# Rotary halves exchanged by ScalarE copies instead of a TensorE rotation matmul, in the first block of a two-block model

## The reference, cut to what matters

```
def rope(x, pos):
    d = x.shape[-1]
    ...
    x1, x2 = jnp.split(x, 2, axis=-1)
    return jnp.concatenate([x1 * cos - x2 * sin, x2 * cos + x1 * sin], axis=-1)
```

## Time and profile before

| what | value |
|---|---|
| median of 3 runs | 2612.03 us (2608.58 to 2612.68) |
| the profiled execution | 2606.96 us, of it 2605.2 us span |
| TensorE busy | 94% of the span |
| VectorE, ScalarE, GpSimd busy | 70%, 51%, 16% |
| weights and the rest read from HBM | 362.60 MB |

### The profile page before, as it was taken

How to read it: one execution, slowest core, us unless ns; L and a number is a source line. 1 busy time by engine, 2 the same in 40 slices (tenths; PEclk the granted TensorE clock), 3 DMA queues, 4 the chain that set the end, 5 groups by cost and what they waited for, 6 DMA issues and landing times.

```text
span 2605.2 us, 50262 instructions
## 1 busy us (share of the span) xinstructions
PE 2459.5 (94%) x18862; PEld 2339.8 (90%) x18862; DVE 1817.3 (70%) x3451; ACT 1333.6 (51%) x2218; POOL 419.9 (16%) x548
## 2 busy tenths in 40 slices
PE   7999998999999999998999998999999988999998
PEld 6998997888999998997888998888999988889998
DVE  5698855666875689856676774876766558667664
ACT  5644455755544644455755545544444454344443
POOL 0000003617930000003526940000000000000000
PEclk9999998999999999999999998988999999899999
DMA  5432342344554433342334554432545543334553
GB/s 208 161 107 100 112 147 88 114 138 146 170 171 156 167 113 109 106 146 98 114 133 151 171 178 138 146 114 90 170 158 182 186 140 128 101 118 146 195 186 130
DMA packets 100432, 366.76 MB, mean 141 GB/s; under 512 B 11632, under 2 KB 12144, under 8 KB 99824
## 3 DMA queue, kind: packets, MB, share of 16 engines
q1 hardware_dynamic: 100208, 363.69, 41.8%
HBM read 362.60 MB, written 1.05 MB: 140 GB/s over the span
## 4 chain that ended last, share of the span: by engine, by line
PE 58%; DVE 18%; POOL 9%; DVEq 5%; ACT 4%; issue 3%; ACTq 1%; DMA 1%; SPq 0%; POOLq 0%
PE psum L450 58%; POOL ring_lo L1963 9%; DVE ring_lo L1282 4%; ACT arena L852 2%; ACT ring_hi L865 1%; DVE arena L1316 1%; DVE arena L1324 1%; DMA ring<-w 1%; DVEq L1757 1%; DVE arena_r L1270 1%; DVEq L1262 1%; DVE arena_r L1268 1%; PE psum L527 1%; DVE arena L1414 1%; DVEq L1439 1%
## 5 line engine op out<-in xcount | busy, mean ns | idle before, releaser
L450 PE MATMUL psum<-hn_hi,ring_hi 128*128 128x272 f32 (+2 forms) x3936 | 1169.4, 298 | 46.6 <-ACT hn_hi L852 20.4
L450 PE MATMUL psum<-hn_hi,ring_lo 128*128 128x272 f32 (+2 forms) x3936 | 1138.3, 290 | 0.0
L450 PE MATMUL psum<-hn_lo,ring_hi 128*128 128x272 f32 (+2 forms) x3936 | 1103.4, 288 | 0.0
L450 PEld LDWEIGHTS psum<-hn_hi,ring_hi 128*128 128x128 f32 x3936 | 767.5, 195 | 79.8 <-issue 54.6
L865 ACT ACTIVATE ring_hi<-ring 128x1024 fp32r<-128x1024 f32 x684 | 715.0, 1055 | 231.0 <-DMA ring<-w 200.5
L1282 DVE TENSOR_TENSOR ring_lo<-ring,ring_hi 128x1024 fp32r<-128x1024 f32 x548 | 668.3, 1228 | 225.5 <-ACT ring_hi L865 187.0
L450 PEld LDWEIGHTS psum<-hn_hi,ring_lo 128*128 128x128 f32 x3936 | 767.3, 195 | 0.0
L450 PEld LDWEIGHTS psum<-hn_lo,ring_hi 128*128 128x128 f32 x3936 | 746.8, 193 | 1.7
L852 ACT ACTIVATE arena<-psum 128x272 f32<-128x272 f32 (+10 forms) x722 | 251.5, 366 | 707.9 <-PE psum L450 598.9
L1963 POOL TENSOR_TENSOR ring_lo<-ring,ring_hi 128x256 fp32r<-128x256 f32 x544 | 419.7, 808 | 1104.7 <-ACT ring_hi L865 1104.7
L450 PE MATMUL psum<-arena_r,ring_hi 128*128 128x256 f32 (+2 forms) x2996 | 555.2, 286 | 20.5 <-DVEq L1262 10.1
(11 more groups left out here) (154 smaller groups left out, 1463.7 us busy)
## 6 DMA issues: line engine op xcount, KB each, us to landing
ring<-w SPq DMA_DIRECT2D x684, 512.0 KB, 3.3
cst<-consts SPq DMA_DIRECT2D x1, 2120.0 KB, 14.6
x_sb<-x_meta SPq DMA_DIRECT2D x1, 1088.0 KB, 4.9
out<-x_sb SPq DMA_DIRECT2D x1, 1024.0 KB, 4.8
arena<-lam SPq DMA_DIRECT2D x1, 256.0 KB, 4.0
par_sb<-par SPq DMA_DIRECT2D x1, 193.0 KB, 4.8
pos_sb<-positions SPq DMA_DIRECT2D x1, 128.0 KB, 6.4
cst<-consts SPq DMA_DIRECT2D x1, 65.5 KB, 5.0
```

The source lines that it names most:

```text
L450: i = nc.tensor.matmul(out_, lhsT=lhsT, rhs=rhs, start=first, stop=last)
```

## The change

For a q/k tile, ScalarE now copies each half of the bank into the place of the other half in the destination (`RQ`, `RK`, `DQ`, `DK`) before it copies the bank to `XS`: two copies of 64x272 for a retention tile, four of 32x272 for a differential attention tile. VectorE multiplies the destination by sin in place, from SBUF, and adds x times cos. The sign of the rotation moves into the sine tables. TensorE has no `turn` for these tiles, no bank is taken for them, and the two rotation matrices leave the constants (128 KB less in the second DMA of constants, 1992 KB for 2120 KB).

```
+            def exchange_halves(key, ps):
+
+                kind, h = key
+                dst, _, _, d = ROT[kind]
+                for at in range(0, P, d):
+                    for a, b in ((at, at + d // 2), (at + d // 2, at)):
+                        op(dst[a:a + d // 2, h, :], ps[b:b + d // 2, :], ACT.Copy)
...
             def stage(key):
...
                         act.wait_ge(*(b1.full(two + ("turned",)) if two[0] in VALUES else s1["taken"].upto(two)))
+                    if kind in ROT:
+                        exchange_halves(key, ps)
                     op(XS[:, s1_slot[key], :], ps, ACT.Copy, b1.free(key))
...
             def turn(key):
 
                 kind, h = key
-                if kind in ROT:
-                    pe.wait_ge(*s1["staged"].upto(key))
-                    scores(b1, (kind, h, "turned"), [(slice(0, P), slice(0, T1), ROT[kind][3], XS[:, s1_slot[key], :])])
-                elif kind in VALUES:
+                if kind in VALUES:
...
                     V.tensor_tensor(TMP[:, 0, :], x, cos, ALU.mult)
-                    dve.wait_ge(*b1.full((kind, h, "turned")))
-                    V.tensor_tensor(TMP[:, 1, :], b1.of((kind, h, "turned"))[:, 0:T1], sin, ALU.mult)\
-                        .then_inc(*b1.free((kind, h, "turned")))
+                    V.tensor_tensor(dst[:, h, :], dst[:, h, :], sin, ALU.mult)
                     V.drain()
-                    V.tensor_tensor(dst[:, h, :], TMP[:, 0, :], TMP[:, 1, :], ALU.add)
+                    V.tensor_tensor(dst[:, h, :], dst[:, h, :], TMP[:, 0, :], ALU.add)
                     fence(s1["taken"].done(key))
...
-    put("sinR", np.sin(angles(128, 1)))
+    half = lambda d: np.where(np.arange(P) % d < d // 2, -1.0, 1.0)[:, None]
+    put("sinR", half(128) * np.sin(angles(128, 1)))
...
-    put("sinD", np.sin(angles(64, 2)))
-    put("rotR", rotation(128, [0]))
-    put("rotD", rotation(64, [0, 64]))
+    put("sinD", half(64) * np.sin(angles(64, 2)))
```

More of the change, by code:

```diff
@@ L81 @@
 _at = 0
-for _name, _n in [("ones", P), ("invM", 1), ("eps", 1), ("one", 1), ("cosR", T1), ("sinR", T1), ("cosD", T1), ("sinD", T1), ("rotR", P), ("rotD", P), ("rotM", P),
+for _name, _n in [("ones", P), ("invM", 1), ("eps", 1), ("one", 1), ("cosR", T1), ("sinR", T1), ("cosD", T1), ("sinD", T1), ("rotM", P),
                   ("retD", RET_HEADS * T1), ("lvl", 6 * P), ("causal", 3 * P), ("ident", P),
@@ L274, in program @@
         cosR, sinR, cosD, sinD = const("cosR"), const("sinR"), const("cosD"), const("sinD")
-        rotR, rotD, rotM = const("rotR"), const("rotD"), const("rotM")
+        rotM = const("rotM")
         ident, ones, ones64 = const("ident"), const("ones"), const("ones64")
@@ L322, in program @@
         VT = {"h": (HV, 0), "r": (RV, 32), "d": (DV, 64)}
-        ROT = {"rq": (RQ, cosR, sinR, rotR), "rk": (RK, cosR, sinR, rotR),
-               "dq": (DQ, cosD, sinD, rotD), "dk": (DK, cosD, sinD, rotD)}
+        ROT = {"rq": (RQ, cosR, sinR, P), "rk": (RK, cosR, sinR, P), "dq": (DQ, cosD, sinD, P // 2), "dk": (DK, cosD, sinD, P // 2)}
         lb_sb, b = view(setup_at, 2 * KT)
```

## The result

The changed kernel took 2620.17 us (median of 6 runs, 2617.3 to 2623.62) beside 2610.68 us of the kernel before (6 runs, 2608.25 to 2612.68). The ratio is 1.0037, 95% interval 1.0024 to 1.005: slower by 9.5 us, outside the range given. The profiled execution took 2618.78 us, 2617.0 of it its span.

The account below looks back on a forecast made before the run. VectorE was taken to set the pace of heads 1 to 6, TensorE that of head 7. Rotations -2.8 and head 0's copies +1.6 made -1.2 us: 2612.03 to 2610.8 us, called the same, range 2604.5 to 2618.

Parts of the forecast that it names:

- Rotations: -1.4 us per layer in head 7: Removing head 7's three rotation matmuls at 0.46 us each saves TensorE 1.4 us per layer, 2.8 us in all.
- One copy 0.40 us: Each ScalarE exchange copy takes 0.40 us: 0.8 us in a retention stage, 1.6 us in a differential attention stage.
- Rival A: Slower: ScalarE late for VectorE's factors in heads 3 to 6 if a copy takes 0.52 us; +5.8, 2617.8 us; chance 0.08.
- Head 0: +0.8 us per layer: Two copies of f1 ahead of the exponentials delay VectorE's factors in head 0 by 0.8 us per layer, 1.6 in all.
- The settle: 0: VectorE's settle gains nothing from the sine product reading SBUF: 0.44 us from PSUM, 0.44 us for the cosine product beside it.
- rival D: Faster: the sine product 0.07 us cheaper from SBUF, 48 times, 3.4 us in all, giving 2607.4 us; chance 0.07.
- Heads 3 to 6: 0, with 0.15 us of cover: Exponentials behind f0's and f1's copies end at 241.64 us, factors start at 241.79 us: just in time, cost 0.
- B: Slower: TensorE's longer wait per head drops its clock before the level products, three times per layer; 5.1 us, 2615.9 us; chance 0.09.

Follow-up runs that it names:

- without copies and rotations: The change without its exchange copies, the sine multiplying the tile itself, so the rotation is left out of the result; ratio 1.001 to the kernel before.
- the repeat: The changed kernel run once more, unaltered, in the second group of runs; ratio 1.0036 to the kernel before.
- idle matmuls: The change with a useless product of the same size and a small one of 16 columns in each rotation's place and bank; ratio 1.0027 to the kernel before.
- both cures: The change with the next head's exponentials ahead of the staging of f1 and useless products in each rotation's place; ratio 1.0019 to the kernel before.
- copies and rotations: The kernel before with ScalarE's 160 exchange copies added, their results overwritten, and TensorE's 48 rotation matmuls kept; ratio 1.0018 to the kernel before.
- the exponentials first in the kernel before: The kernel before with the next head's exponentials staged earlier on ScalarE, ahead of the staging of f1; ratio 1.0024.
- the change with the exponentials first: The change with the next head's exponentials ahead of the staging of f1 on ScalarE; ratio 1.0012 to the kernel before.
- the exchange in heads 0 and 7: The kernel before with ScalarE's exchange for only six tiles, staged in each layer's first and last head, and the exponentials first; ratio 0.9999.
- slabs on GpSimd: Two of VectorE's five slabs' low parts per head given to GpSimd: kernel before 1.0088, change 1.0171, change with the next head's exponentials ahead of f1's staging 1.0047.

## Why the prediction was wrong, point by point

- *Rotations: -1.4 us per layer in head 7.* Right: 22.18 us by the window, against 23.55, and TensorE full in both. In heads 1 to 6 the time became a wait of 2.3 us, as written.
- *One copy 0.40 us.* Right: two copies and the staging copy take 1.21 us, four and the staging copy 2.00 us. Rival A's own condition, 0.42 us a copy, wasn't met.
- *Head 0: +0.8 us per layer.* Measured +0.56. VectorE waits 1.16 us for its factors where it waited 0.34, which is the 0.8; head 0 as a whole grew by less. The prediction also has head 0's rotations followed by a wait of TensorE. The earlier trace rows show TensorE busy in all of head 0's 23.12 us, and without copies and rotations head 0 is 0.26 us shorter.
- *The settle: 0.* Right. The sine product takes 436 ns on average with both inputs in SBUF and took 433 with one in PSUM, so rival D falls. The rule of the Trainium skill ("VectorE: DVE Perf Modes", the TRN2 errata's table) falls with it for this shape: nothing of the estimated 65 ns per operation is seen.
- *Heads 3 to 6: 0, with 0.15 us of cover.* **This step failed.** The cover was computed with TensorE's times of the kernel before. In the changed kernel TensorE delivers f0 after level products that take 1.49 us longer, and 0.15 us covers nothing of it. The sum put 0 where 4 x 1.49 = 6 us per layer could be lost; the two profiles of the change have 6.1, 5.3, 4.9 and 5.2 us.
- *The rivals A and B as separate cases.* This is the same error. B was right in its mechanism, and right even in its count of three falls a layer, each followed by a shorter wait, for a kernel without the copies; but there the heads grew by 1.2 and 0.4 us, where B had 2.55 per layer. A was right in its place, but with the clock full the copies cost 0.8 us. Together they cost 6.6 and 5.9. With the copies VectorE gets late too, TensorE's next wait stays at 2.3 us or more, and the clock falls again: four falls, little of them absorbed. Each rival was priced in the world of the forecast, where the other's slack still existed.
- *The range.* Its lower end is a slip of the sum, 2607.4 - 3.4 = 2604.0 and not 2604.4; nothing hangs on it.

The sum by what was measured is 12.5 us in the seven heads less 2 x 1.37 in head 7, +9.7 us; the runs gave +9.5. In the repeat it is 11.2 - 2.7 = +8.4 us, and the runs gave +10.4. So the first agreement is in part luck.

**Still open.** The variants measure more than their heads account for. With idle matmuls the seven heads take 2.6 us more, and head 7 takes 24.57 us for 23.55, since the idle pairs are dearer than the rotations: 4.6 us of the 7 us that the runs show. With both cures it is 3.4 of 5 us, with copies and rotations 1.7 of 4.7, with the exponentials first in the kernel before 1.4 of 6. Where head 7 is shorter, the runs show less of it: the change with the exponentials first should be 0.9 us faster than before and is 3.1 slower, without copies and rotations 1.0 faster and is 2.6 slower, the exchange in heads 0 and 7 3.6 faster and is 0.3 faster. So 1.5 to 5 us lie outside the heads, always to the slower side. A part can be the clock outside the heads. In the runs with the exponentials first in the kernel before the granted clock is 0.967 on average, beside 0.970, with no fall in the profiled heads. Over 2610 us that is some 8 us of clock, where one fall of 3.4 us at half loses 1.7. With copies and rotations it is 0.9695, or 1.3 us, too little for the 3 us open there. Two profiles of before differ by 3 us there too. Why the clock should fall more often outside the heads wasn't tried.

## What to carry to other kernels

When a change thins the cover in one place and lengthens a wait in another, follow the chain from the one to the other: if it closes into a loop through the engines, the slack is shared and the two costs must be priced together. A cover of 0.15 us is not a zero; work out what the sum becomes if the engine that feeds it comes 1 us later. A filler that is to stand in for removed work has to be timed too: these idle matmuls took 0.80 us for 0.46. Taking work off an engine that isn't the bound can cost time, since its longer wait can cost it the clock for the very products that the bound is waiting for.

## What the runs showed of the hardware

- TensorE's clock fell to its lower level after four waits of 2.29 to 2.78 us ahead of narrow matmuls in the first layer of the changed kernel, and not after two others of 2.34 and 2.40 us there; without copies and rotations it fell after 2.28, 2.64 and 1.64 us and not after 2.33 and 1.69. The length of the wait alone doesn't decide it. One fall cost 1.49 us in 52 matmuls (6.73 against 5.24 us).
- ScalarE's copies to other partitions start 0.40 us apart and don't overlap, also with 64 partitions in place of 32 (1.21 us for three), where copies that keep their partitions start 0.27 us apart. A copy of half as many partitions was no cheaper.
- With slabs on GpSimd some of VectorE's operations between SBUF tiles stretch: 0.17 us became 0.63 for a 128x16 product behind the factors, 0.29 became 0.75 for a 128x128 one, 0.45 became 0.70 for the factors of 128x272, while those of 128x256 kept their 0.42. The sum of VectorE's time rose in the kernel before with the slabs, though 17 us of slabs were taken off. The Trainium skill has the rule ("SBUF — State Buffer", the section on the two separate sides): VectorE operations with two SBUF inputs and GpSimd's operations exclude each other for a whole instruction. These rows agree in kind: GpSimd's pieces take 0.89 us each, and the operations grow by 0.25 to 0.47 us on average. Only one of the three expectations named it.
